# Decay products behind weight subtractions, half a pooled tile among the inverse's corners, first state's zeros and gate sums in front

## The reference

```python
h = rms_norm(x, attn_norm); z = h @ w_in
z_pool = z[..., :1024]; zs = token_shift(z[..., 1024:], mu_shift)
d = causal_multiscale_pool(z_pool)                 # windows 2, 4, 8, 16
pool_out = einsum('btgc,gcd->btgd', d, pool_w) * pool_scale
w = -softplus(-(w0 + tanh(zw) @ w_up)) - 0.5; decay = exp(-exp(w))
kk = k * k_k / norm; k = k * (1 + (a - 1) * k_a)
S = S * w_t + (S @ a_t) b_t + v_t k_t; y = S r_t    # over 256 tokens, 16 heads of 64
...
x = x + relu(h2 @ w_ffn_up)**2 @ w_ffn_down
gate = sigmoid(rms_norm(x, ple_norm) @ w_ple_gate)
x = x + gate * (p @ w_ple_proj)
x = rms_norm(x, final_norm)                        # then the second layer starts:
n = rms_norm(x, attn_norm_g_2); proj = n @ w_in_2  # gated linear attention first
```

## Time and profile before

| | |
|---|---|
| median of 3 timed runs | 2287.65 us (2287.09 to 2288.55) |
| profiled execution, its own time | 2290.27 us |
| its span, first to last instruction | 2288.5 us |
| TensorE busy | 2266.2 us, 99% |
| VectorE busy | 1458.3 us, 64% |
| ScalarE busy | 978.5 us, 43% |
| mean granted TensorE clock | 0.998 |
| chain that ended last | TensorE 92%, VectorE 6%, ScalarE 1% |

### The profile page before, as it was taken

One profiled execution on the slowest core, in us unless ns is written; L12 is line 12 of the kernel. 1 busy time (PEld: TensorE's weight loads), 2 busy tenths in 40 slices (PEclk: granted clock), 3 DMA queues, 4 the chain that ended last, 5 costly groups with the idle time before them and its releaser, 6 DMA issues.

```text
span 2288.5 us, 34500 instructions
## 1 busy us (share of the span) xinstructions
PE 2266.2 (99%) x15676; PEld 2057.7 (90%) x15676; DVE 1458.3 (64%) x1214; ACT 978.5 (43%) x929; POOL 177.8 (8%) x138
## 2 busy tenths in 40 slices
PE   9999999999999999999999999999999999999999
PEld 8998988998998988988889999888998998999898
DVE  6699676665664665565558559786665665565564
ACT  5653245433333333344544364475343433433432
POOL 1004110010110110110000001100000000001000
PEclk9999999999999999999999999999999999999999
DMA  8553166656656656666556655345555655665644
GB/s 252 173 164 88 33 222 207 200 205 199 205 200 204 199 206 197 208 223 209 176 178 195 186 187 148 111 151 184 185 197 197 225 190 184 221 209 178 226 161 147
DMA packets 335306, 425.06 MB, mean 186 GB/s; under 512 B 4521, under 2 KB 249625, under 8 KB 334777
## 3 DMA queue, kind: packets, MB, share of 16 engines
q1 hardware_dynamic: 333465, 418.50, 56.3%
q0 software_dynamic: 1552, 4.23, 0.6%
q10 hardware_dynamic: 144, 0.13, 0.0%
HBM read 420.75 MB, written 2.10 MB: 185 GB/s over the span
## 4 chain that ended last, share of the span: by engine, by line
PE 92%; DVE 6%; ACT 1%; issue 0%; DMA 0%; DVEq 0%; SPq 0%; ACTq 0%
PE PS L673 50%; PE PS L719 23%; PE PS L721 11%; PE PS L937 1%; DVE ring_r L2197 1%; PE PS L718 1%; PE PS L738 1%; PE PS L1129 1%; DVE ring_r L2532 1%; PE PS L856 0%; ACT arena_r L1527 0%; PE PS L1010 0%; PE PS L1065 0%; PE PS L1057 0%; PE PS L1319 0%
## 5 line engine op out<-in xcount | busy, mean ns | idle before, releaser
L1527 ACT ACTIVATE arena_r<-ring 128x2048 fp32r<-128x2048 f32 (+1 forms) x394 | 690.1, 1760 | 940.7 <-PE PS L673 542.3
L2139 DVE TENSOR_TENSOR ring_r<-ring,arena_r 128x2048 fp32r<-128x2048 f32 x316 | 721.6, 2290 | 489.7 <-ACT arena_r L1527 489.7
L719 PE MATMUL PS<-arena_r,arena_r 128*128 128x512 f32 x2432 | 789.7, 382 | 0.0
L673 PE MATMUL PS<-arena_r,arena_r 128*128 128x512 f32 (+2 forms) x2128 | 707.5, 346 | 1.7 <-DVE ring_r L2532 0.9
L721 PE MATMUL PS<-arena_r,ring_r 128*128 128x256 f32 x2280 | 621.5, 273 | 0.0
L673 PE MATMUL PS<-ring_r,arena_r 128*128 128x512 f32 (+1 forms) x1504 | 523.3, 361 | 1.2 <-DVE ring_r L2197 1.2
L719 PEld LDWEIGHTS PS<-arena_r,arena_r 128*128 128x128 f32 x2432 | 449.1, 189 | 56.3
L673 PE MATMUL PS<-arena_r,actT_r 128*128 128x512 f32 (+1 forms) x1184 | 442.1, 373 | 0.0
L673 PEld LDWEIGHTS PS<-arena_r,arena_r 128*128 128x128 f32 (+1 forms) x2128 | 401.5, 189 | 44.1 <-issue 4.8
L721 PEld LDWEIGHTS PS<-arena_r,ring_r 128*128 128x128 f32 x2280 | 437.4, 192 | 3.9
L673 PEld LDWEIGHTS PS<-ring_r,arena_r 128*128 128x128 f32 x1504 | 277.5, 190 | 35.7 <-issue 3.1
(11 more groups left out here) (381 smaller groups left out, 1648.5 us busy)
## 6 DMA issues: line engine op xcount, KB each, us to landing
ring<-in_w_ffn_up SPq DMA_DIRECT2D x32, 2048.0 KB, 9.6
ring<-in_w_ffn_down SPq DMA_DIRECT2D x32, 2048.0 KB, 7.9
ring<-in_w_in SPq DMA_DIRECT2D x22, 2048.0 KB, 8.3
ring<-in_w_gate SPq DMA_DIRECT2D x22, 2048.0 KB, 8.1
ring<-in_w_up SPq DMA_DIRECT2D x22, 2048.0 KB, 8.2
ring<-in_w_in SPq DMA_DIRECT2D x32, 1024.0 KB, 5.2
ring<-in_w_out SPq DMA_DIRECT2D x16, 2048.0 KB, 9.1
ring<-in_w_down SPq DMA_DIRECT2D x12, 2048.0 KB, 8.1
```

The source lines that it names most:

```text
L673: mm = pe.matmul(dst, r32(w, early)[rows], r32(x, early)[rows], start=first and q == 0, stop=last and q == 2)
L719: mm = pe.matmul(dst, r32(wh[:, k, c]), r32(beside(high, low)), start=x == 0, stop=x == KT - 1)
L1527: return act.activation(dst, src, ACT.Copy, scale=scale)
L2139: v.tensor_tensor(r32(u), u, high_of(high_home(n, i, j)), ALU.subtract).then_inc(S["w_low"], counts(units, j))
```

## The change

On TensorE the first half of pooled tile 4 is split: four of its eight slices stand ahead of the first corner products, four between the two turns of v. On VectorE, in the head, the three decay products (with a wait that is long fulfilled) move from ahead of low1(5,2) to behind low1(6,0), the subtractions low1(6,1) to low1(6,3) each move one product forward; in level 3 the turns of all four groups come after all four adds; the zeros of the first state move from behind the last corner copies to ahead of them, with a wait for the turns (they write where the turned matrix was read). At the gate, the subtraction of unit (50,2) moves behind the two gate sums and `tokens_low`, that of (50,3) from right behind the sums to behind `rms("n4")`; ScalarE does `tokens_high` before the squares. Nothing is added or removed but the wait for `dt_turned`.

```diff
@@ TensorE
+        pool_tile(2 + (len(LEVELS) - 1) // 2, 0, range(4))
         for g in range(2):
             pe.wait_ge(S["d_added"], 4 * (len(LEVELS) - 2) + 2 * g + 2)
             corner_group(g, INV[g], LATE, ...).then_inc(S["f_ready"], 1)
         pe.wait_ge(S["shifted"], 3)
-        for c in range(2):
-            turn_v(c)
-        pool_half(len(LEVELS) - 1)
+        turn_v(0)
+        pool_tile(2 + (len(LEVELS) - 1) // 2, 0, range(4, 8))
+        turn_v(1)
@@ ScalarE, first block of N_GLA
             if c == 0:
-                norm_chunk("n4", None, 3)
+                tokens_high("n4", None, 3)
+                squares("n4", 3)
                 for q in range(4):
                     scaled_squares(q)
                 root("n4")
@@ VectorE, head
         link(v.tensor_tensor(kk, kk, tmp1, ALU.mult))
-        v.wait_ge(S["head_acts"], 3)
-        (the three decay products)
         low1(5, 2)
...
         low1(6, 0)
+        v.wait_ge(S["head_acts"], 3)
+        (the three decay products)
+        low1(6, 1)
         v.tensor_tensor(ga, kk, ga, ALU.mult)
         v.wait_ge(S["rkr_ready"], 1)
         v.tensor_tensor(AR[:, :, :, C:P], chunks(zr), chunks(lw), ALU.mult).then_inc(S["ar_ready"], 1)
-        low1(6, 1)
+        low1(6, 2)
         v.wait_ge(S["ar_ready"], 1)
         for e in range(2):
             h = HALF[e]
             v.tensor_tensor(BK[h, :, :, e * C:(e + 1) * C], ...)
-            low1(6, 2 + e)
+            if e == 0:
+                low1(6, 3)
             ins = v.tensor_tensor(BK[h, :, :, (1 - e) * C:(2 - e) * C], ...)
@@ VectorE, levels
             block_added(lv, 1)
-            block_turned(lv, 0)
+            if lv < len(LEVELS) - 2:
+                block_turned(lv, 0)
             block_added(lv, 2)
-            block_turned(lv, 1)
+            if lv < len(LEVELS) - 2:
+                block_turned(lv, 1)
             block_added(lv, 3)
-            block_turned(lv, 2)
-            block_turned(lv, 3)
+            for g in range(2 if lv < len(LEVELS) - 2 else 0, 4):
+                block_turned(lv, g)
@@ VectorE, corners
         low1(8, 1)
+        v.wait_ge(S["dt_turned"], 4 * (len(LEVELS) - 1))
+        v.memset(SD[0], 0.0)
+        for e in range(2):
+            v.memset(UV(0)[HALF[e], :, e, :], 0.0).then_inc(S[f"s_placed{e}"], 1)
         for g in range(2):
             v.wait_ge(S["corner_ready"], g + 1)
             (two copies to DTi)
-        v.memset(SD[0], 0.0)
-        for e in range(2):
-            v.memset(UV(0)[HALF[e], :, e, :], 0.0).then_inc(S[f"s_placed{e}"], 1)
@@ VectorE, gate, c = 0 to 3
-            low(n + 1, (0, 1, 2))
+            low(n + 1, (0, 1, 2) if c < 3 else (0, 1))
@@ VectorE, N_GLA, c = 0 to 3
-            low(n, (3,))
+            if c:
+                low(n, (3,))
             if c == 0:
                 tokens_low("n4", None, 3)
+                low(n, (2,))
                 for q in range(4):
                     scale_residual(q)
                 link(rms("n4", rs_fin))
+                low(n, (3,))
                 v.wait_ge(S["chunk_summed"], SUMMED["scaled"])
```

More of the change, by code:

```diff
@@ L2275, in _, with chunks @@
         low1(6, 0)
+        def chunks(a):
+            return a.rearrange("p m (c j) -> p m c j", c=NCH)
+        v.wait_ge(S["head_acts"], 3)
+        lwc, kkc = (a.rearrange("p m (c j) -> p (m c) j", c=NCH) for a in (lw, kk))
+        arf = AR.rearrange("p m c j -> p (m c) j")
+        v.tensor_copy(PEND.rearrange("p m c -> p (m c)"), lwc[:, :, C - 1])
+        v.tensor_scalar(arf[:, :, 0:1], kkc[:, :, 0:1], -1.0, None, ALU.mult)
+        v.scalar_tensor_tensor(arf[:, :, 1:C], lwc[:, :, 0:C - 1], -1.0, kkc[:, :, 1:C], ALU.mult, ALU.mult)
+        low1(6, 1)
         v.tensor_tensor(ga, kk, ga, ALU.mult)
         v.wait_ge(S["rkr_ready"], 1)
-        def chunks(a):
-            return a.rearrange("p m (c j) -> p m c j", c=NCH)
         v.tensor_tensor(AR[:, :, :, C:P], chunks(zr), chunks(lw), ALU.mult).then_inc(S["ar_ready"], 1)
-        low1(6, 1)
+        low1(6, 2)
         v.wait_ge(S["ar_ready"], 1)
```

## The result

The changed kernel takes a median of 2292.96 us over ten runs (2291.28 to 2294.26), beside 2287.48 for the kernel before: ratio 1.0023, 95% interval 1.0015 to 1.0032. It is 5.5 us slower. The forecast was 2288.8 with a range up to 2292.1, so the time lies outside the range, on the slow side. The profiled execution took 2294.26 us, 1.3 above its kernel's median, with a span of 2292.4: only 3.9 us more than the span of before, whose profiled execution stood 2.8 above its own. Two executions among the experiments, one of before (2934.34 us) and one of c_corners (2603.14), ran at a mean clock of 0.75 and 0.85 and are left out of the ratios and comparisons; the medians don't hang on them.

The account below looks back on a forecast made before the run. TensorE, busy 2266.2 of 2288.5 us, was taken to bound the kernel. Head +1.6, corners -4.85, gate +2.95 and clock +1.4 gave +1.1 on the median 2287.65: 2288.8 us, range 2285.7 to 2292.1.

Parts of the forecast that it names:

- The -4.85 of the corners: From level 3 to the first state product: pauses and 3.05 us of half clock go, L1020 starts 4.85 us earlier.
- the gate: At the gate sums: net +2.95 us for the late subtraction of unit 3, and +1.4 for the clock behind it.
- the head: At BK's transposes (L884): VectorE's later copy delays TensorE and the masking, +1.6 us, bounds +0.5 to +2.2.
- sees wide matmuls first: At the corners: twelve pooled matmuls in front let the clock meet wide matmuls first, avoiding 3.05 us of half clock.
- the clock's term: After the gate's pause TensorE's clock falls, costing 1.4 us, bounds 0 and 3.05.
- the 4.8 us pause: At L673 TensorE waits 4.8 us before unit 3 for the subtraction queued behind the reciprocal.
- 2.95: At the gate: net loss in us from unit 3's late subtraction, before any clock loss.
- Rival (d): VectorE is in time at the gate and the head costs its lower bound: -5.4 us, 2282.3; chance 8%.
- the 1.05 of L738: At the gate, earlier sums cut TensorE's wait at L738 from 1.4 to 0.4 us, winning 1.05.
- Rival (c): Half clock in full at both the corners and the gate: +5.8 us, 2293.4; chance 12%.
- (a): The clock keeps its full rate after the gate's pause: -0.3 us, 2287.35; chance 25%.
- (b): The corners still run partly at 1.2 GHz: about +2.2 us on the sum, 2291; chance 15%.

Follow-up runs that it names:

- c_corners: Kernel before with the corner part alone (pooled half split, turns after adds, zeros ahead of the corner copies): 2285.61 us, ratio 0.9990.
- a_gate: Kernel before with the gate part alone (both subtractions moved behind, tokens ahead of the squares): 2292.95 us, ratio 1.0023.
- e_filled: a_gate with 40 matmuls, never read, filling TensorE's pause ahead of unit 3: 2290.68 us, ratio 1.0018 against before.
- f_headlate: b_head with low1(7,0) moved behind VectorE's three copies of turned BK: 2287.06 us, ratio 0.9999 against before.
- g_zeros: Kernel before with only the three memsets of the first state moved ahead of the corner copies: 2286.18 us, ratio 0.9995.
- b_head: Kernel before with the head part alone (decay products behind low1(6,0), subtractions one product forward): 2289.88 us, ratio 1.0009.
- i_all: Changed kernel with f_headlate's edit in the head and d_repaired's at the gate: 2283.90 us, ratio 0.9985 against before.
- d_repaired: Kernel before with corner and gate parts, unit 3's subtraction ahead of the reciprocal, one residual product ahead of the low tiles: 2284.26 us, ratio 0.9984.
- h_split: Kernel before with TensorE's corner order alone (pooled half split, four slices in front, four between turns): 2286.45 us, ratio 0.9996.
- j_unit3: Changed kernel with unit 3's subtraction moved one line up, ahead of the reciprocal: 2287.69 us, ratio 1.0000 against before.

## Why the prediction was wrong, step by step

**Where the profiled sum was put: the step that failed most.** The prediction summed differences inside the profiled span of before and put the sum on the median, though it had noted that the profiled execution took 2.6 us more than the median. The -4.85 of the corners contains 3.05 of half clock. That loss was in the profiled execution and, by the traces of a_gate, e_filled, f_headlate and g_zeros with the same order and by the times and clocks above, not in the median one; it can't be won back from a time that doesn't contain it. The corner part alone measured -1.7; -4.85 + 3.05 is -1.8. That the 3.05 are about the 2.6 between profiled and median execution was to be seen before the forecast. Measured part by part, the corners missed their term by 3.15, the gate by 1.3 and the head by 1.0, less the 1.05 by which the parts don't add up: the 4.4 between +1.1 and +5.5.

**The corners inside the trace: right.** Predicted 12.9 us from level 3 to the first state product, measured 13.1; no 0.96 pause, a second pause of 0.3 to 1.0 (measured 0.37), the zeros hidden. TensorE's timeline of the changed kernel:

```profile
251.02 2.21 PE L955 MATMUL PS<-arena 32*32 32x32 f32 x128
...
254.32 0.68 PE L944 MATMUL PS<-cst,arena 64*64 64x64 f32 x14 [0.37 <-issue]
```

The reason given for the clock, that it "sees wide matmuls first", isn't borne out: with the old order it fell in two of six traces (before and b_head, against a_gate, e_filled, f_headlate and g_zeros), with the new one in one of six (i_all, against after, c_corners, d_repaired, h_split and j_unit3). That is too few to tell the orders apart.

**The gate: the mechanism right, the clock's term mis-sized.** The wait at L738 (0.4), the late reciprocal, the 4.8 us pause (measured 4.6), the half clock behind it: all as told. On the clock of the changed kernel everything comes 1.74 earlier: the subtraction ends at 1202.16, predicted 1203.9, since the head and corners had shifted the gate. But the clock cost 2.84, not 1.4 (in a_gate's trace 8.52 - 5.50, 3.02). The value between the bounds was chosen by an argument (one pause and wide matmuls lose less than two pauses and small ones) for which no row stood; the nearest row, 3.05, was the better price. 2.95 + 2.84 is 5.8, the trace shows 5.9 and the gate alone 5.65. Rival (d) took a gate in time at the 1.05 of L738; by the prediction's own times (unit 3 at 1199.1 instead of 1200.95) it is 1.85, and the repaired gate gave 1.35.

The Trainium skill, "TensorE: Matmul & The Clock Gate", section "What's actually happening", has the half rate as the default and activity as what releases it; by that rule the loss was certain. The trace agrees: the granted clock went to 0.50 just before 1201.2, while TensorE was idle, in a_gate's at 1200.2, and stayed at 1.00 in the trace with the pause filled.

**The head: the mechanism right, the sum short.** The new wait at L884 was put at 2.3 and is 2.1; the copies start at 177.96 (predicted 177.8); the mask comes 2.0 late, not 1.6. Ahead of it the wait at L856 didn't fall to 1.0 but rose to 1.5, and VectorE spent most of the 2.38 us that it got free waiting for ScalarE's copies (1.34 before low1(5,2), 0.86 before low1(5,3)). What no step had is the half clock at 194 to 197. Inside the chain it cost 0.6 on 16 score products (1.76, against 1.16 at 179.71) and 1.0 on the pooled half (3.87 against 2.88), of which 1.15 reached L937, 3.15 late in all. In j_unit3's trace, with the same head and no half clock at 194, L937 starts at 213.06, only 2.08 late. The head alone measured +2.6 in the median.

**The sum.** The terms of the prediction, those of the trace of after, and those of the parts alone:

| | predicted | trace | parts alone, median |
|---|---|---|---|
| head | +1.6 | +3.15 | +2.6 |
| corners | -4.85 | -4.7 | -1.7 |
| gate, wait and clock | +4.35 | +5.9 | +5.65 |
| sum | +1.1 | +4.35 | +6.55 |
| whole, measured | | +3.9 | +5.5 |

The trace's terms stand beside the 4.1 by which L775 was late and the 3.9 of the span; 0.25 more is a pause among the inverse's products, 1.41 before and 1.15 after. The medians of the parts add to 1.05 more than the whole; that is within what the intervals leave open, and isn't settled. Rival (c) named 2293.4, close to the 2292.96 measured, but that was luck, by another mechanism: it had the corners at half clock, and they ran at full. Of it only the gate's half came. Rivals (a) and (b) named a full clock at the gate and a half clock at the corners, neither of which came; (d) fell with the reciprocal's place behind ScalarE's squares.

## What to carry to other kernels

Before gains are read from a profile, ask how far the profiled execution stands from the median of the timed ones, and take out of the sum each loss that only it may have: here a stretch at half clock that wasn't behind a long pause was such a loss. When work is moved to an in-order queue's other side of a wait for a second engine, compute when that wait ends and who needs the moved work first: one subtraction behind one reciprocal cost 5.3 of 5.5 us. Here a pause of TensorE of 4.6 us cost its own length and 2.8 to 3.0 more in clock.

## What the runs showed of the hardware that was not expected

**Short pauses and the clock.** Granted clocks in these stretches were 1.00 or 0.50. A pause of 4.6 us brought the lower level in both traces that have it. The length of pauses of about 1 us among small matmuls doesn't decide it: g_zeros had 0.95 and 1.19 and kept 1.00, before had 0.96 and 0.31 and fell to 0.50, and b_head fell with 0.74 and 0.24. What decides is open. So is the fall in the head: with the 2.1 us wait at L884 it fell in three of three traces, at 194 in two and just before 180 in the third,

```profile
179.70:182.60 2.90, 2.90 (x21) 2.61 (x21) 0.90 (x3) 2.72 (x8) 0.00 (x0) 0.50 0.00 0
```

(window of j_unit3, right behind the wait), and in none of the nine traces without that wait. The falls at 194 came 0.2 to 0.4 us after TensorE resumed from a second mask wait of some 1.2 (191.42 and 193.77 in the head's timeline). Those two mask waits alone don't bring it: before and the six kernels with its head have them too and kept 1.00. So in these traces the fall goes with the L884 wait, but how the two act together isn't known.

**Pauses that nothing ended.** They stand a fixed number of instructions apart: in the earlier trace rows the first is behind 30 corner matmuls, and then come 98 and, in the row of 34 behind the second pause, the rest of 64 turns, so 30 before it: 128 matmuls, 256 instructions with their weight loads. In the new order 12 more matmuls stand ahead, and the second pause comes 12 turns sooner, behind 18 instead of 30 (the row of 14 that is left of the first turn, in the changed kernel and in h_split). Their length varies: 0.96, 0.95 and, in a_gate, 0.74 at the first place; 0.31 and 1.19 at the second. Twelve wide matmuls ahead of the corners hid the first one in all six traces with that order.

The Trainium skill, "Runtime: NRT & Kernel Launch", section "Instruction fetch mechanics", says that instructions come in blocks of 256 and that crossing a block is mostly hidden. The spacing agrees; for matmuls of 32 to 64 columns the hiding doesn't, with up to 1.2 us in these rows. That the pauses are fetches is argued from the spacing, and was not tried by itself.
